# A four-mixer decoder trunk on one core: untransformed input rows transposed as they land, the norm's root moved behind the first products, shorter filler

## What is computed

```python
def _rmsnorm(x, gain):
    y = xf * lax.rsqrt(jnp.mean(xf * xf, axis=-1, keepdims=True) + NORM_EPS)
    return y * gain
proj = h @ w_in                      # h = rmsnorm(x); q, k, v, g are its columns
scores = jnp.einsum('bhncd,bhned->bhnce', q, k) * decay[:, None]
y_intra = jnp.einsum('bhnce,bhnev->bhncv', scores, v)
y = (y - mu) * lax.rsqrt(var + NORM_EPS)        # per head
y = y * gn_gain * jax.nn.silu(g)
return y @ w_out
```

## Time and profile before

| | |
|---|---|
| median of 3 runs | 1593.15 us (1592.84 to 1593.97) |
| the profiled execution | 1591.9 us |
| its span, first to last instruction | 1589.7 us |
| busy in the span | PE 1569.7 (99%), DVE 1212.1 (76%), ACT 984.6 (62%), POOL 264.4 (17%) |
| matmuls | 9522 |
| HBM | 461.23 MB read, 300 GB/s over the span |

### The profile page before, as it was taken

One profiled execution on the slowest core, in us unless ns is written; L12 is line 12 of the kernel. 1 busy time (PEld: TensorE's weight loads), 2 busy tenths in 40 slices (PEclk: granted clock), 3 DMA queues, 4 the chain that ended last, 5 costly groups with the idle time before them and its releaser, 6 DMA issues.

```text
span 1589.7 us, 23667 instructions
## 1 busy us (share of the span) xinstructions
PE 1569.7 (99%) x9522; PEld 1310.1 (82%) x9522; DVE 1212.1 (76%) x811; ACT 984.6 (62%) x731; POOL 264.4 (17%) x244
## 2 busy tenths in 40 slices
PE   8999999999999999999999999999999999999997
PEld 7888889999988778888888888888888888888886
DVE  5556566655557758888888888888888888888897
ACT  6444445333454356777777777777777777777775
POOL 5599215300036107100000000000000000000100
PEclk9999999999999999999999999999999999999999
DMA  9544648865511286999999999999999999999993
GB/s 350 165 157 158 211 139 283 281 201 186 186 54 56 78 309 242 395 385 363 386 354 366 395 366 352 388 360 368 382 379 347 389 376 344 393 372 349 399 393 150
DMA packets 202144, 469.19 MB, mean 295 GB/s; under 512 B 7785, under 2 KB 20289, under 8 KB 202065
## 3 DMA queue, kind: packets, MB, share of 16 engines
q1 hardware_dynamic: 199872, 461.13, 80.0%
q0 software_dynamic: 2048, 6.88, 1.5%
q10 hardware_dynamic: 144, 0.07, 0.0%
HBM read 461.23 MB, written 15.21 MB: 300 GB/s over the span
## 4 chain that ended last, share of the span: by engine, by line
PE 66%; DVE 1%; ACT 1%; issue 1%; POOL 0%; ACTq 0%; POOLq 0%; DVEq 0%
PE PS L1713 63%; PE PS L1832 2%; PE PS L2171 0%; ACT c_padded L878 0%; ACT weights_hi L878 0%; PE PS L2014 0%; POOL states L798 0%; DVE scan L1254 0%; DVE states L1254 0%; DVE weights_lo L1254 0%; PE PS L2129 0%; DVE scan_tmp L1254 0%; DVE residual L1254 0%; DVE normed_rows L1706 0%; DVE scan L1480 0%
## 5 line engine op out<-in xcount | busy, mean ns | idle before, releaser
L1254 DVE TENSOR_TENSOR weights_lo<-weights_raw,weights_hi 128x2048 fp32r<-128x2048 f32 (+1 forms) x419 | 964.3, 2310 | 263.7 <-ACT weights_hi L878 261.8
L878 ACT ACTIVATE weights_hi<-weights_raw 128x2048 fp32r<-128x2048 f32 (+1 forms) x419 | 800.7, 1912 | 366.4 <-PE PS L1713 354.0
L1713 PE MATMUL PS<-weights_hi,gathered_hi 128*128 128x512 f32 x896 | 355.3, 397 | 0.3 <-DVE gathered_lo L1594 0.3
L1713 PE MATMUL PS<-weights_hi,gathered_lo 128*128 128x512 f32 x896 | 355.0, 396 | 0.0
L1713 PE MATMUL PS<-weights_lo,gathered_hi 128*128 128x512 f32 x896 | 352.3, 393 | 0.0
L1713 PE MATMUL PS<-weights_hi,act_transposed_hi 128*128 128x512 f32 x624 | 252.9, 405 | 0.5 <-DVE act_transposed_lo L1402 0.5
L1713 PE MATMUL PS<-weights_hi,act_transposed_lo 128*128 128x512 f32 x624 | 247.0, 396 | 0.0
L1713 PE MATMUL PS<-weights_lo,act_transposed_hi 128*128 128x512 f32 x624 | 245.7, 394 | 0.0
L1713 PEld LDWEIGHTS PS<-weights_hi,gathered_lo 128*128 128x128 f32 x896 | 168.2, 188 | 41.3
L1713 PEld LDWEIGHTS PS<-weights_lo,gathered_hi 128*128 128x128 f32 x896 | 168.2, 188 | 41.1
L1713 PEld LDWEIGHTS PS<-weights_hi,gathered_hi 128*128 128x128 f32 x896 | 168.2, 188 | 39.9 <-DVE gathered_lo L1594 0.3
(11 more groups left out here) (279 smaller groups left out, 1273.6 us busy)
## 6 DMA issues: line engine op xcount, KB each, us to landing
weights_raw<-in_moe_w_up SPq DMA_DIRECT2D x111, 1024.0 KB, 7.3
weights_raw<-in_moe_w_down SPq DMA_DIRECT2D x111, 1024.0 KB, 7.0
weights_raw<-in_moe_w_gate SPq DMA_DIRECT2D x110, 1024.0 KB, 7.3
weights_raw<-in_ret_w_in SPq DMA_DIRECT2D x24, 1024.0 KB, 6.7
weights_raw<-in_ffn_w_gate SPq DMA_DIRECT2D x14, 1024.0 KB, 5.1
weights_raw<-in_ffn_w_up SPq DMA_DIRECT2D x14, 1024.0 KB, 5.1
weights_raw<-in_ffn_w_down SPq DMA_DIRECT2D x14, 1024.0 KB, 5.0
weights_raw<-in_ret_w_out SPq DMA_DIRECT2D x8, 1024.0 KB, 4.9
```

The source lines that it names most:

```text
L878: return nc.scalar.activation(o, i, ACT.Copy)
L1254: return nc.vector.tensor_tensor(o, a, b, op)
L1713: return nc.tensor.matmul(o, l, r, start=start, stop=stop)
```

## The change

1. Head: PE begins on a constant tile that DVE sets, `plain_x` transposes x as it lands, `norm()` and both makers of `hn` are gone. The splits of x banks 0 and 1 move ahead of those of weight unit 0. `first_unit` multiplies by the first half of unit 0 before the second half is split. Idle products stand behind each wait.
2. The root: VectorE makes a diagonal of r and r squared; PE turns r into a row behind unit 1. q is multiplied by the row (DVE, was ACT's copy), v by r squared (DVE, two instructions, was one copy), g inside silu (ACT, two instructions, was one).
3. `yt_lo` is signalled for halves; the last head's output product waits for the first half only.
4. Filler: 13 to 10 after the last head, 16 to 9 before the dense layer, 6 to 3 in S5, 5 to 2 in the router.
5. `x_ready` asks for one bank rather than two at the starts of retention and S5.
6. `s5_out`: direct terms of both parts first, then all real states, then all imaginary ones, each with its own wait.
7. The split of unit MOE_U0 + 1 on DVE moves behind `pick`; the sum of squares of tile 1 moves from ACT to DVE.

The diff, cut to its core (new semaphores, the tile `rstd_sq` and the counts of `hn0_ready` and `hn1_ready` on POOL are left out):

```diff
 ACT
                 nc.scalar.activation(std[:, :], ssq[:, :], ACT.Sqrt, scale=1.0 / D, bias=eps).then_inc(std_done, 1)
-                act.wait_ge(rstd_done, 1)
-                nc.scalar.activation(hn[:, 1, :], resid[:, 1, :], ACT.Copy, scale=rstd[:, 1:2]).then_inc(hn1_ready, 1)
...
             copy(gains[:, :], PS[:, 7, 0:7 * KT]).then_inc(gains_ready, 1)
+            norm_split(0, range(2))
             act.wait_ge(landed[0], 16)
             copy(w_hi[:, 0, 0:UNIT // 2], raw[:, 0, 0:UNIT // 2]).then_inc(first_hi_half, 1)
             copy(w_hi[:, 0, UNIT // 2:UNIT], raw[:, 0, UNIT // 2:UNIT]).then_inc(hi_ready, 1)
-            norm_split(0)
+            norm_split(0, range(2, KT // 2))
             split_hi(1)
...
+            def gate_silu():
+                act.wait_ge(rstd_done, 1)
+                for t in range(TT):
+                    ins = nc.scalar.activation(gated[:, t, :], PS[:, t, :], ACT.Silu, scale=rstd[:, t:t + 1])
+                ins.then_inc(g_silu, 1)
...
-                        copy(qk_t[:, :, :, :], PS[:, 0:2, :].rearrange("p a (b c) -> p a b c", b=2)).then_inc(qk_copied, 1)
+                        copy(qk_t[:, 1, :, :], PS[:, 1, :].rearrange("p (b c) -> p b c", b=2)).then_inc(qk_copied, 1)
...
-            act.wait_ge(resid_ready, 3)
-            nc.scalar.activation(hn[:, 1, :], resid[:, 1, :], ACT.Square, accum_out=ssq[:, 1:2]).then_inc(ssq1_done, 1)
 DVE
-                nc.vector.tensor_scalar(hn[:, 0, :], resid[:, 0, :], rstd[:, 0:1], None, ALU.mult).then_inc(hn0_ready, 1)
+                for t in range(TT):
+                    nc.vector.tensor_scalar(act_rows[:, t, 0:P], ident, rstd[:, t:t + 1], None, ALU.mult)
+                tt(rstd_sq[:, :], rstd[:, :], rstd[:, :], ALU.mult).then_inc(rstd_sq_ready, 1)
...
+            nc.vector.memset(act_rows[:, 0, SEQ:SEQ + P], 1.0).then_inc(warm_ready, 1)
             norm_rows()
+            norm_split(0, range(2))
             dve.wait_ge(first_hi_half, 1)
...
-            norm_split(0)
+            norm_split(0, range(2, KT // 2))
             split_lo(1)
+
+            def take_v():
+                dve.wait_ge(rstd_sq_ready, 1)
+                for t in range(TT):
+                    ins = nc.vector.tensor_scalar(v_rows[:, t, :], PS[:, 2 + t, :], rstd_sq[:, t:t + 1], None, ALU.mult)
+                ins.then_inc(v_copied, 1)
...
-                ins.then_inc(yt_lo, 1)
+                    if ft % 2:
+                        ins.then_inc(yt_lo, 1)
...
+                    if n == f0 + 4:
+                        if h == 0:
+                            dve.wait_ge(first_row_done, 1)
+                            link(nc.vector.tensor_copy(rstd_row[:, :], PS[:, 6, 0:SEQ]))
+                        dve.wait_ge(used, f0 + 1)
+                        query, row = by_token(PS[:, 0, :], 2)
+                        tt(qk_t[:, 0, :, :], query, row, ALU.mult).then_inc(q_scaled, 1)
...
-            for i in range(2):
-                split_lo(MOE_U0 + i)
+            split_lo(MOE_U0)
...
+            dve.wait_ge(resid_ready, 3)
+            nc.vector.scalar_tensor_tensor(out=hn[:, 1, :], in0=resid[:, 1, :], scalar=1.0, in1=resid[:, 1, :],
+                                           op0=ALU.mult, op1=ALU.mult, accum_out=ssq[:, 1:2]).then_inc(ssq1_done, 1)
...
             ins.then_inc(pick_ready, 1)
 
+            split_lo(MOE_U0 + 1)
 PE
-                    pe.wait_ge(xlo_ready, KT // 2 * i + max(2, kt // 2 + 1))
+                    pe.wait_ge(xlo_ready, KT // 2 * i + max(2 if i == 1 else 1, kt // 2 + 1))
...
+            pe.wait_ge(warm_ready, 1)
+            for _ in range(6):
+                mm(PS[:, 5, 0:P], act_rows[:, 0, SEQ:SEQ + P], act_rows[:, 0, SEQ:SEQ + P], True, True)
             pe.wait_ge(c_landed, 16)
-            idle_work(6, 5)
+            plain_x()
             pe.wait_ge(g_landed, 64)
             nc.tensor.transpose(PS[:, 7, 0:7 * KT], gain_rows[0:7 * KT, :],
                                 cst[0:7 * KT, C_IDENT:C_IDENT + 7 * KT]).then_inc(gains_t, 1)
-            idle_work(6, 5)
-            pe.wait_ge(std_done, 1)
-            idle_work(4, 5)
-            norm()
             idle_work(4, 5)
             pe.wait_ge(xhi_ready, 1)
             idle_work(3, 5)
+            pe.wait_ge(xhi_ready, 2)
+            idle_work(3, 5)
+            pe.wait_ge(first_hi_half, 1)
+            idle_work(3, 5)
+
+            def first_unit():
+                for half in range(2):
+                    if half:
+                        split_ready(0)
+                    else:
+                        pe.wait_ge(first_lo_half, 1)
+                    for j in range(2):
+                        for kt in range(4 * half, 4 * half + 4):
+                            x_ready(0, kt)
...
             def head_out(h, half, n):
+                pe.wait_ge(yt_lo, 2 * h + half + 1)
                 if half == 0:
-                    pe.wait_ge(yt_lo, h + 1)
...
                 cols_unit(f0 + 1, 1)
+                if h == 0:
+                    pe.wait_ge(rstd_sq_ready, 1)
+                    pe.wait_ge(c2_landed, 16)
+                    for t in range(TT):
+                        ins = mm(PS[:, 6, t * P:(t + 1) * P], ones, act_rows[:, t, 0:P], True, True)
+                    ins.then_inc(first_row_done, 1)
...
                 pe.wait_ge(qk_copied, h + 1)
+                pe.wait_ge(q_scaled, h + 1)
...
             idle_work(10, 0)
-            pe.wait_ge(yt_hi, HEADS)
-            idle_work(3, 0)
             head_out(HEADS - 1, 0, RET_UNITS - 2)
+            pe.wait_ge(yt_lo, 2 * HEADS)
...
-            idle_work(16, 4)
+            idle_work(9, 4)
...
-                pe.wait_ge(st_re_ready, q + 1)
-                if q == QUARTERS - 1:
-                    pe.wait_ge(last_im_ready, 1)
-                else:
-                    pe.wait_ge(st_im_ready, q + 1)
...
-                    for l in range(STEP):
-                        for j in range(2):
+                for j in range(2):
+                    if j == 0:
+                        pe.wait_ge(st_re_ready, q + 1)
+                    elif q == QUARTERS - 1:
+                        pe.wait_ge(last_im_ready, 1)
+                    else:
+                        pe.wait_ge(st_im_ready, q + 1)
+                    for a in range(QKT):
+                        for l in range(STEP):
...
-                    idle_work(6, 5)
+                    idle_work(3, 5)
...
-                    idle_work(5, 4)
+                    idle_work(2, 4)
```

More of the change, by code:

```diff
@@ L1023, in _ @@
                             act.wait_ge(y_normed, h - 1)
-                        nc.scalar.activation(gated[:, :, :], PS[:, 0:2, :], ACT.Silu).then_inc(g_silu, 1)
+                        gate_silu()
                     if h == 1 and n == f0 + 2:
@@ L1964, in _ @@
                     pe.wait_ge(g_silu, h)
-                cols_unit(f0, 0, 0 if h == 0 else None)
+                if h:
+                    cols_unit(f0, 0)
+                else:
+                    first_unit()
                 if h:
```

53 lines of the change are left out of this document (34 added, 19 removed).

## The result

The changed kernel takes 1582.0 us (median of 6 runs, 1581.64 to 1583.19), the kernel before 1592.76 in the same session (6 runs, 1591.63 to 1593.97). The ratio is 0.9935 [0.9924, 0.9945]: 10.8 us faster, where 7.1 were forecast. The profiled execution took 1582.01 us, its span is 1580.2.

The account below looks back on a forecast made before the run. TensorE was taken as the bound, busy 1569.7 of 1589.7 us. Terms 2.0 - 0.1 + 0.8 + 1.1 + 0.4 + 1.2 + 1.7 = 7.1 us gave 1586.1 us, range 1583.8 to 1590.0.

Parts of the forecast that it names:

- The head, 2.0 less 0.1: Kernel start: root and normed rows leave the chain, gaining 2.0 us; root on q, v and g costs 0.1.
- the fast case: Head: the earlier start also brings the full clock forward; first product at 12.0 us, gain 2.3.
- the slow one: Head: sixteen transposes run at half speed; first product at 12.7 us, gain 1.6.
- After the last head 0.8: Last head's output product waits for two low parts instead of four, with ten idle products; gain 0.8 us.
- before the dense layer 1.1: Dense layer's start: nine idle products instead of sixteen, two banks needed; starts at 224.4 instead of 225.55, gain 1.1 us.
- bank of x 0.4: S5's start: waiting for one bank instead of two removes the 0.44 us wait before 470.27; gain 0.4.
- GLU, router, gather 1.7: Last GLU half to first expert: moved split, square on DVE and fewer router idle products gain 1.7 us, bounds 1.0 and 1.9.
- S5, 1.2: S5 outputs: `s5_out` waits placed behind the direct terms remove 0.22 us at 496.86 and 0.95 at 545.89; together 1.2.
- I cost them at nothing: S5 quarter 0: three fewer idle products save 0.7 us, but an equal wait on POOL's padded rows replaces them; gain 0.
- The clock did not fall where filler was cut: Rival, chance 0.20: clock falls where filler was cut, 1.65 us per half-clock stretch; one gives 1587.8, two 1589.4.
- would add 1.1 to 1.65: S5 at 495 us: the half-clock stretch there can also vanish, adding 1.1 to 1.65 us to the gain.
- The three others: Head bound by parameter chain, 1587.1, chance 0.08; later gains become waits, 1590.2, 0.08; expert unit 7's transfer late, 1597.4, 0.04.

Follow-up runs that it names:

- the transfer held back: Kernel before, with a weight unit's transfer on SyncE waiting until the output of S5's quarter 0 is done; 1591.14 against 1592.05 us, ratio 0.9996.
- the grouping alone: Kernel before, with direct terms of both tiles first in `s5_out`, state products of both behind, both waits still in front; 1592.17 us, ratio 0.9997.
- the fillers alone: Kernel before, with last head's low half signalled by two banks, one bank of x, and idle products 13 to 10, 16 to 9, 6 to 3; 1587.27 us.

## Why the prediction missed

**The head, 2.0 less 0.1: right, with some luck.** Alone 2.0 by the medians, 11.95 and 12.80 for a forecast of 12.0 and 12.7. Behind it the gain was 0.4 to 0.5 smaller than the two cases forecast (2.3 and 1.6, less 0.1): at the start of head 1 it is 1.84 in the fast case (59.61 against 61.45) and 0.97 in the slow one. The 2.0 contain 0.4 us outside the span, which no term had. What chooses between the cases was left open. Of seven profiles with six products on the constant tile, two show the sixteen transposes at 3.67 and 3.68 us, both begun at 4.73 behind a wait of 0.71, and five at 2.8 or less; with eight products none of five took more than 3.05. The rule of the Trainium skill ("TensorE: Matmul & The Clock Gate", "Part 1: The HAM clock gate") that activity releases the clock agrees with the 2.47, since the kernel before reached the full level only later than 7.37 us (0.35 for the gains' transpose, 0.27 in the fast case). The hole before the constants, 0.71 in the two slow profiles and 0.51 to 0.57 in the others with six products, may be the reason of the 3.67; the profiles are too few to show it.

**After the last head 0.8, before the dense layer 1.1, bank of x 0.4: right** (0.78, 1.15 and 0.30 at the landmarks). The bank gave 0.7 at S5's first product (466.67 against 470.27), and 0.4 of it went again before the next unit, where TensorE waits for VectorE's diagonal of the root.

**GLU, router, gather 1.7: right.** 1.22 at the transposes, 0.70 at the logits, 2.05 alone. DVE's split behind `pick` and the later transfer cost nothing that shows: from the transposes to the first expert it is 13.32 instead of 14.02, and the experts have no wait.

**S5, 1.2: wrong, and this is the step that failed.** Between 470.27 and 550.90 of the kernel before, it was 0.22 + 0.95 for the waits, and they came. But from the transposes of quarter 1 (485.96) to 550.90 the trace gained 3.87 us, and 0.52 more at the stall behind it. Three things were left out.

First, "I cost them at nothing", of the three idle products in quarter 0. The reasoning on the wait was right to 0.15 us and the conclusion wrong by 1.1 (put back) to 1.9 (alone): TensorE's instructions go on arriving in a wait for data, while idle products use them up and move the place in the list where a packet is needed.

Second, the stalls under "issue". The waits of the kernel before listed them, 0.6 us, and I had passed over them because nothing in the profile releases them. The largest one was not even there to be read: the stretch of lower clock lay over it. Up to 503.02 it was worth 1.14 us (6.16 against 5.02 with the transfer held back). The other two cost 0.2 more than their brackets of 0.27 and 0.35, which begin at the modelled end of the product before. Counted from start to start it is 0.47 at 493.61 (1.43 from 492.18 for 31 products, where the changed kernel takes 3.96 for 128) and 0.52 at 551.75 (0.85 from the product before to this one, 0.33 after): 2.1 together.

Third, the price of the order of `s5_out`, which I never set. Keeping the 48 direct products together and the 128 state products behind them takes two changes of shape out of each quarter, 0.25 us, 1.0 in all. The four quarters in the changed kernel and the three undisturbed ones of the grouping alone show it; the medians of the grouping alone don't (0.3, within the noise). The Trainium skill has the rule ("TensorEngine Tiling (Array Packing)", "Key Properties": changing the tiling mode drains the engine); these runs give 0.12 us a change, and don't show whether a drain is what takes it. Looked up beforehand, it would have given a term of the sum.

From 482.76 to 543.83 the trace gained 3.87: 0.25 + 1.01 by the waits, 0.47 + 1.14 by the stalls, 1.0 by the grouping. The third stall, 0.52, lies behind it. To my sum of 7.1 all this adds 3.2, the slow case of the head takes 0.9 away, the bank of x 0.1, and the GLU adds 0.2: 9.5, where the trace has 9.51, and 0.4 outside the span makes the 9.9 between the two profiled executions. The medians lie 0.9 further apart, which is within what single executions differ by. And of the 4.1 us between the forecast time and 1582.0, 0.4 is the kernel before itself: 1592.76 here, where the forecast started from 1593.15.

**The rivals.** The clock did not fall where filler was cut. The stretch at 495 vanished, as the text allowed, but "would add 1.1 to 1.65" has the wrong reason: without the lower clock the kernel before is no faster. The three others did not happen. The range failed at its lower end because neither the stalls nor the grouping were a term of it.

## What to carry to other kernels

A wait that the profile puts under "issue" in a stretch of very short products can be a wait for instructions, as it was here: compare it with the packets of the instruction queue, and with the transfers that run at that hour. In such a stretch filler is not free even where a wait of the same length takes its place, and parts measured one by one sum to more than the whole, since each can remove the same stall. Count TensorE's instructions up to a stall in two kernels: the same count in both says that instructions are what is missing. Keep products of one array shape together.

## What the runs showed of the hardware that was not expected

A packet of 16 KB of instructions took 0.9 to 1.6 us on the DMA engines, and TensorE went on 1.2 to 1.6 us after it had landed. One weight unit of 1 MB, 3.6 us long, delayed it by about 2 us (500.11 instead of 498.12).

The stalls stood behind the same number of recorded products in every kernel with the same head (3657, or 3654 with the new one), whichever product that was.

Half the clock for 3.4 us cost nothing in the kernel before, since the next instructions were not there sooner; for 6.8 us, in the profile of the order of `s5_out` alone, it stretched the output of quarter 0 to 5.96 us.

Each pair of changes between products on 32 rows by 32 columns and on 128 rows by 32 columns costs 0.25 us.

Where the 0.4 us outside the span come from stays open. Around the span there are 2.2 us in the kernel before and with the order of `s5_out` or the fillers alone, 1.95 with the edit of the GLU alone and 1.8 with the head alone, in every run of each within 0.15.
